# The opening transfers of a two-block transformer kernel, issued in another order and from other queues

## The chip, the cores and the metric

One core of one Trainium2 chip runs the whole program in one launch. The metric is the device time in microseconds (us); lower is better. The engines are TensorE (PE; its weight loads are listed as PEld), VectorE (DVE), ScalarE (ACT), GpSimd (POOL) and SyncE (SP). SP, ACT and POOL can issue DMA transfers; in the profile queue 1 is SP's, queue 10 is ACT's, queue 0 is POOL's.

## The reference

The input x is 256 rows of 1024 float32. Two blocks are applied to it: one with an attention layer beside a state-space mixer ("even"), a stick-breaking attention layer and two feed-forward layers, and one with a feed-forward layer, a gated and dilated mixing layer, cross attention to a memory and a last feed-forward layer. Only the first steps matter here:

```python
hn = rmsnorm(x, even_norm[i])
proj = hn @ even_w_in[i]                       # [256, 1024] @ [1024, 1280]
q, k, v, u = split(proj, ...)                  # u: the state-space mixer's input, 512 wide
# state-space mixer, G = 32 groups, N = 64 states, P = 16 channels
dt  = exp(log_dt)[:, None]
mag = exp(a_re * dt)
lam_re, lam_im = mag * cos(a_im * dt), mag * sin(a_im * dt)
bb_re, bb_im = (complex weight from lam and a) * (b_re, b_im)
h = associative_scan(lam, einsum(u, bb))       # over the 256 positions
y = einsum(h_re, c_re) - einsum(h_im, c_im)
```

## The kernel before, in words

Every engine has an instruction stream of its own, written out by hand, and they meet at semaphores. Matrices come from HBM in 1 MB "units" (128 partitions x 2048 float32) into `raw`, which has three buffers; `load` (L558 to L566) issues unit u on SP once buffer u mod 3 is free. The units of `even_w_in` are u0 to u0+4: columns 3 and 4 (the mixer's u), then 0, 1 and 2 (q, k, v).

SP (L552 on) issues x in one transfer (L554, semaphore `x_loaded`), the early constants with the identity (L555, 157.5 KB), the norm's gain (L556), units 0 to 2 (L622 to L623 through L566), 20 small loads (L625, `small_in`) and then units 3 and 4, which have to wait until TensorE is through with units 0 and 1. ACT (L1781 on) begins with seven transfers: `ssm_loads` (a_re, a_im and log_dt, which is broadcast to 128 partitions, 16 KB), `b_loads` (two matrices of 256 KB with what is broadcast, to partitions 0 to 63 of `bc_nat`) and `c_loads` (two of 128 KB, to partitions 64 to 127).

The opening computation: VectorE sums the squares of row half 0 of x (t = 0, L2221), ScalarE those of row half 1 (L1673), GpSimd makes the reciprocal roots (L1565, L1567), one row half after the other, once its memsets (L1542, L1544) are done. VectorE scales row half 0 (L2232) and half of row half 1 (L2234), ScalarE the other half (L1693). Ahead of that last scaling ScalarE waits for `ssm_in` and takes exp(log_dt) (L1792), from which VectorE makes the mixer's tables (L2439 on).

TensorE (L958 on) works in this order: it waits for the constants and for all three of `ssm_in`, flips a_re and a_im (L806), flips the scaled rows (`norm(0)`, 16 flips at L806), from which ScalarE makes `h_whole` (L1701); waits for `b_in` and flips B (32 flips at L806); multiplies unit 0 (`whole_t`, L713); waits for `c_in` and flips C (L982); multiplies unit 1 (L713); then flips and groups u, multiplies units 2 to 4 (L725) between the mixer's steps, and so on:

```python
norm(0)
pe.wait_ge(b_in, 16 * 2)
...
whole_t(u0, OUT["even_u0"], fresh=chunks(0))
pe.wait_ge(c_in, 16 * 2)
...
whole_t(u0 + 1, OUT["even_u1"])
```

VectorE copies the flipped B (L2451), and then works without long waits on the mixer's V and W products (L2481 to L2509); TensorE needs the last of them for the K product (L1061). GpSimd adds the skip term to it (L1590) and then SP, ACT and POOL move it in small transfers inside SBUF (L517) ahead of the convolution (L1098, L1101).

## Time and profile before

| | |
|---|---|
| median of three runs | 1208.72 us |
| lowest, highest | 1207.64, 1209.81 us |
| profiled execution: span from first to last instruction | 1208.6 us |
| busy: PE, DVE, ACT, POOL | 98%, 65%, 49%, 6% |
| unit 0: issued, landed | 2.27, 16.67 us |
| TensorE's first matmul on unit 0 | 16.71 us |

The profile is of one execution, whose whole time is given by its span alone. Times in its rows count from the first instruction. A busy TensorE isn't TensorE at its peak, since matmuls are pipelined; what a change is worth is read from the waits and from the chain of work that ended last. In a row of the timeline or of the groups, "out<-in" are the tiles written and read, xN is the number of instructions, and the bracket at the end is the idle time before them with what ended it.

### The profile page before, as it was taken

To read this page: it belongs to the slowest core of one execution; us is meant where nothing else is said; L and a number is where in the kernel's file an instruction comes from. 1 tells how busy PE (TensorE), PEld (TensorE's weight loads), DVE (VectorE), ACT (ScalarE), POOL (GpSimd) and SP (SyncE) were. 2 spreads that over 40 slices of the span, in tenths; PEclk is the share of its full clock that TensorE was granted. 3 is DMA by queue.
4 is the path that set the end of the run, shared out by engine and by line. 5 is a ranking of instruction groups with operands and counts; after the bars stand their busy time and mean duration, and the time that the engine had idled before them with its cause. 6 is when DMAs were issued, how large, how long until landed. Compare 5 with 4: busy or idle time off the path is not lost.

```text
span 1208.6 us, 17835 instructions
## 1 busy us (share of the span) xinstructions
PE 1185.3 (98%) x7139; PEld 1026.1 (85%) x7139; DVE 783.1 (65%) x848; ACT 588.8 (49%) x730; POOL 67.1 (6%) x87
## 2 busy tenths in 40 slices
PE   6999999999999999999999999999999999999997
PEld 5876888888999988888888888888889988888886
DVE  6956676666755557666667666667594646766665
ACT  4547643434566645434345444445574545443443
POOL 2120000000002110000000000000011000000000
PEclk9999999999999999999999999999999999999999
DMA  7254565656544355656555556565543534656561
GB/s 196 92 145 141 162 207 177 200 179 202 180 140 168 113 168 181 207 177 196 185 191 168 199 178 205 177 204 175 175 133 116 183 127 134 197 185 197 179 202 70
DMA packets 156104, 205.81 MB, mean 170 GB/s; under 512 B 7752, under 2 KB 129168, under 8 KB 156048
## 3 DMA queue, kind: packets, MB, share of 16 engines
q1 hardware_dynamic: 154944, 203.30, 52.2%
q10 hardware_dynamic: 944, 1.52, 0.6%
q8 instruction: 40, 0.66, 0.2%
q0 software_dynamic: 160, 0.20, 0.1%
q14 instruction: 16, 0.13, 0.0%
HBM read 202.77 MB, written 1.05 MB: 169 GB/s over the span
## 4 chain that ended last, share of the span: by engine, by line
PE 92%; DVE 3%; ACT 2%; DMA 1%; SPq 1%; issue 0%; POOL 0%; POOLq 0%; ACTq 0%
PE outp L754 26%; PE outp L695 20%; PE acc L695 20%; PE outp L758 14%; PE acc L806 3%; PE outp L713 1%; DMA raw<-in_even_w_in_dram 1%; PE outp L1193 1%; DVE w_lo L2198 1%; PE outp L725 1%; DVE h_pair L2243 1%; PE outp L860 1%; SPq L517 1%; PE acc L1173 1%; ACT w_hi L1650 0%; ACT h_pair L1711 0%
## 5 line engine op out<-in xcount | busy, mean ns | idle before, releaser
L1650 ACT ACTIVATE w_hi<-raw 128x2048 fp32r<-128x2048 f32 x177 | 339.4, 1918 | 413.0 <-PE outp L758 283.2
L2198 DVE TENSOR_TENSOR w_lo<-raw,w_hi 128x2048 fp32r<-128x2048 f32 x177 | 405.3, 2290 | 177.0 <-ACT w_hi L1650 176.9
L754 PE MATMUL outp<-h_pair,w_hi 128*128 128x512 f32 x1056 | 253.9, 391 | 0.3
L754 PEld LDWEIGHTS outp<-h_pair,w_hi 128*128 128x128 f32 x1056 | 195.0, 188 | 42.7 <-DVE h_pair L2243 4.2
L758 PEld LDWEIGHTS outp<-h_pair,w_lo 128*128 128x128 f32 x1056 | 135.4, 191 | 5.2
L695 PE MATMUL acc<-w_hi,f_lo 128*128 128x512 f32 x352 | 137.4, 390 | 0.0
L695 PE MATMUL acc<-w_hi,f_hi 128*128 128x512 f32 x352 | 137.4, 390 | 0.0
L695 PE MATMUL acc<-w_lo,f_hi 128*128 128x512 f32 x352 | 137.1, 389 | 0.0
L758 PE MATMUL outp<-h_pair,w_lo 128*128 128x256 f32 x1056 | 137.0, 283 | 0.0
L695 PE MATMUL outp<-w_hi,h_pair 128*128 128x512 f32 (+1 forms) x416 | 113.9, 361 | 0.3 <-DVE w_lo L2198 0.3
L2297 DVE TENSOR_REDUCE arena<-outp 128x256 f32<-128x512 f32 x88 | 56.7, 686 | 58.4 <-PE outp L758 56.2
L2310 DVE TENSOR_REDUCE arena<-outp 128x256 f32<-128x512 f32 x88 | 56.7, 686 | 56.4 <-PE outp L758 56.1
L695 PEld LDWEIGHTS outp<-w_hi,h_pair 128*128 128x128 f32 x416 | 73.1, 189 | 13.4 <-DVE w_lo L2198 1.4
L695 PEld LDWEIGHTS acc<-w_lo,f_hi 128*128 128x128 f32 x352 | 66.1, 188 | 14.0
L695 PEld LDWEIGHTS acc<-w_hi,f_hi 128*128 128x128 f32 x352 | 66.2, 188 | 12.7
L754 PE MATMUL outp<-m_pair,w_hi 128*128 128x512 f32 x320 | 76.7, 392 | 0.0
L695 PEld LDWEIGHTS acc<-w_hi,f_lo 128*128 128x128 f32 x352 | 66.2, 188 | 12.4
L695 PE MATMUL outp<-w_lo,h_pair 128*128 128x512 f32 (+1 forms) x208 | 74.2, 357 | 0.0
L695 PE MATMUL outp<-h_pair,w_hi 128*128 128x256 f32 x384 | 70.8, 286 | 0.0
L754 PEld LDWEIGHTS outp<-m_pair,w_hi 128*128 128x128 f32 x320 | 59.3, 188 | 12.5 <-issue 0.2
L695 PEld LDWEIGHTS outp<-h_pair,w_hi 128*128 128x128 f32 x384 | 59.8, 191 | 0.9 <-issue 0.5
L1565 POOL TENSOR_SCALAR arena<-arena 128x1 f32<-128x1 f32 x20 | 9.6, 481 | 907.3 <-ACT xn L1673 884.8
(340 smaller groups left out, 1438.7 us busy)
## 6 DMA issues: line engine op xcount, KB each, us to landing
raw<-in_ffn_w_gate_dram SPq DMA_DIRECT2D x44, 1024.0 KB, 5.6
raw<-in_ffn_w_up_dram SPq DMA_DIRECT2D x44, 1024.0 KB, 5.6
raw<-in_ffn_w_down_dram SPq DMA_DIRECT2D x44, 1024.0 KB, 4.9
raw<-in_odd_w_in_dram SPq DMA_DIRECT2D x12, 1024.0 KB, 5.2
raw<-in_w_in_dram SPq DMA_DIRECT2D x10, 1024.0 KB, 5.2
raw<-in_even_w_in_dram SPq DMA_DIRECT2D x5, 1024.0 KB, 14.4
raw<-in_even_w_out_dram SPq DMA_DIRECT2D x4, 1024.0 KB, 6.8
raw<-in_cross_wk_dram SPq DMA_DIRECT2D x4, 1024.0 KB, 5.7
```

The source lines that it names most:

```text
L517: eng.dma_start(m_in[PC * j:PC * j + PC, cc, S - 1 - j:, :, :], lags[32 * cc:32 * cc + PC, 0:j + 1, :, :]).then_inc(landed, 16)
L695: ins = nc.tensor.matmul(dst, lhs, rhs, start=start and n == 0, stop=stop_ and n == 2, skip_group_check=skip)
L713: ins = nc.tensor.matmul(outp[:, k % NB, m * L:(m + 1) * L], w[:, c, m * P:(m + 1) * P], h_f32[:, c, :], start=c == 0, stop=c == C - 1)
L725: ins = nc.tensor.matmul(outp[:, k % NB, t * UW:(t + 1) * UW], h_f32[:, c, t * P:(t + 1) * P], w[:, c, :], start=c == 0, stop=c == C - 1)
L754: nc.tensor.matmul(bank, w[0][:, c, m * P:(m + 1) * P], x[:, :, c, :], start=c == 0, stop=c == C - 1, skip_group_check=True)
L758: ins = nc.tensor.matmul(outp[:, (k + m) % NB, 0:L], w[1][:, c, m * P:(m + 1) * P], x[:, 0, c, :], start=False, stop=c == C - 1, skip_grou ...
L806: return nc.tensor.transpose(dst, src, ident[base:base + rows, base:base + rows])
L860: nc.tensor.matmul(outp[:, (k + m) % NB, :].rearrange("p (a l) -> p a l", l=L)[:, :, rows], w[:, c, m * P:(m + 1) * P], m_pair[:, :, c, ro ...
L1650: A(w_hi[:, slot(u), :], raw[:, u % RAW, :], ACT.Copy).then_inc(w_hi_ready, 1)
L2198: tt(w_lo[:, slot(u), :], raw[:, u % RAW, :], w_hi[:, slot(u), :].bitcast(F32), ALU.subtract).then_inc(w_lo_ready, 1)
L2297: V.reduce_sum(silu[:, j % 2, m * L:(m + 1) * L], bank.rearrange("p (a l) -> p l a", l=L), AX).then_inc(out_free[(k + m) % NB], 1)
L2310: V.reduce_sum(b[:, m * L:(m + 1) * L], bank.rearrange("p (a l) -> p l a", l=L), AX).then_inc(out_free[(k + m) % NB], 1)
```

## The change

x comes in two transfers, one for each row half, with a semaphore each; VectorE waits for the first, ScalarE for the second. The B transfers go from ACT's queue to SP's, between units 0 and 1, and the C transfers between units 1 and 2. log_dt gets its own semaphore and is issued by GpSimd ahead of its memsets; TensorE's first wait is then for a_re and a_im only, and ScalarE's wait ahead of the exponential is for log_dt alone. ACT keeps the two issues of a_re and a_im. The computation is the same.

```diff
@@ -355,11 +355,12 @@
         acc_ready = sem("acc_ready")
         acc_free = [sem(f"acc_free{i}") for i in range(NB)]
         out_free = [sem(f"out_free{i}") for i in range(NB)]
-        x_loaded, consts_in, late_in, late2_in, mem_in, fin_in = (sem("x_loaded"), sem("consts_in"), sem("late_in"),
+        x_loaded = [sem(f"x_loaded{t}") for t in range(T)]
+        consts_in, late_in, late2_in, mem_in, fin_in = (sem("consts_in"), sem("late_in"),
                                                                   sem("late2_in"), sem("mem_in"), sem("fin_in"))
         ssm_in, b_in, c_in, small_in, gain0_in = (sem("ssm_in"), sem("b_in"), sem("c_in"), sem("small_in"),
                                                   sem("gain0_in"))
-        bc_flipped = sem("bc_flipped")
+        bc_flipped, dt_in = sem("bc_flipped"), sem("dt_in")
         sum_ready, result_ready = sem("sum_ready"), sem("result_ready")
         act_step, dve_step, pool_step = sem("act_step"), sem("dve_step"), sem("pool_step")
         half_ready = sem("half_ready")
@@ -502,13 +503,13 @@
             return v.rearrange("(a n) -> a n", a=1)
         ssm_loads = [(a_raw[:, j, :, :], a[n][0].unsqueeze(1).to_broadcast([G, 2, N]))
                      for j, n in enumerate(["ssm_a_re", "ssm_a_im"])]
-        ssm_loads += [(log_dt, row(a["ssm_log_dt"][0]).to_broadcast([P, G]))]
         b_loads = [(bc_nat[G * j:G * j + G, :].rearrange("g (h m) -> g h m", h=2),
                      a[n][0].rearrange("g n p -> g (n p)").unsqueeze(1).to_broadcast([G, 2, 1024]))
                     for j, n in enumerate(["ssm_b_re", "ssm_b_im"])]
         c_loads = [(bc_nat[G * j + 64:G * j + 64 + G, 0:N * PC], a[n][0].rearrange("g p n -> g (p n)"))
                    for j, n in enumerate(["ssm_c_re", "ssm_c_im"])]
         SSM = len(ssm_loads)
+        dt_load = (log_dt, row(a["ssm_log_dt"][0]).to_broadcast([P, G]))
         m_moves = [(j, cc) for j in range(S) for cc in range(4)]
         M_SP, M_POOL, M_ACT = m_moves[:15], m_moves[15:20], m_moves[20:]
 
@@ -551,7 +552,8 @@
 
         @block.sync
         def _(sp):
-            sp.dma_start(x_sb[:, :, :], a["x"][0].rearrange("(t p) f -> p t f", p=P)).then_inc(x_loaded, 16)
+            for t in range(T):
+                sp.dma_start(x_sb[:, t, :], a["x"][0, t * P:(t + 1) * P, :]).then_inc(x_loaded[t], 16)
             sp.dma_start(early, a["consts"][:, 0:EARLY_W]).then_inc(consts_in, 16)
             sp.dma_start(gains[:, 0, :], a["even_norm"][0].rearrange("(p c) -> p c", c=C)).then_inc(gain0_in, 16)
 
@@ -619,8 +621,13 @@
             if "even" in running:
                 u0 = UNITS["even"]
                 w = by_p(a["even_w_in"][0])
-                for j, n in enumerate([3, 4, 0]):
-                    load(u0 + j, cols(w, n))
+                load(u0, cols(w, 3))
+                for dst, src in b_loads:
+                    sp.dma_start(dst, src).then_inc(b_in, 16)
+                load(u0 + 1, cols(w, 4))
+                for dst, src in c_loads:
+                    sp.dma_start(dst, src).then_inc(c_in, 16)
+                load(u0 + 2, cols(w, 0))
                 for dst, src in small_loads:
                     sp.dma_start(dst, src).then_inc(small_in, 16)
                 for j, n in enumerate([1, 2]):
@@ -1539,6 +1546,8 @@
         def _(pool):
             own = Own(pool, pool_step)
             gp = nc.gpsimd
+            if "even" in running:
+                gp.dma_start(*dt_load).then_inc(dt_in, 16)
             gp.memset(half, -0.5).then_inc(half_ready, 1)
             if "even" in running:
                 gp.memset(m_in.rearrange("p a b c d -> p (a b c d)"), 0.0).then_inc(kz_ready, 1)
@@ -1782,13 +1791,9 @@
                 u0, k0 = UNITS["even"], OUT["even"] - 2
                 for dst, src in ssm_loads:
                     nc.scalar.dma_start(dst, src).then_inc(ssm_in, 16)
-                for dst, src in b_loads:
-                    nc.scalar.dma_start(dst, src).then_inc(b_in, 16)
-                for dst, src in c_loads:
-                    nc.scalar.dma_start(dst, src).then_inc(c_in, 16)
-                act.wait_ge(x_loaded, 16)
+                act.wait_ge(x_loaded[1], 16)
                 squares(0, x_sb)
-                act.wait_ge(ssm_in, 16 * SSM)
+                act.wait_ge(dt_in, 16)
                 A(small[:, 0, :], log_dt, ACT.Exp).then_inc(dt_ready, 1)
                 norm_rows(0, x_sb)
                 act.wait_ge(lam_mag, 1)
@@ -2423,7 +2428,7 @@
 
             def even():
                 u0, k0 = UNITS["even"], OUT["even"] - 2
-                dve.wait_ge(x_loaded, 16)
+                dve.wait_ge(x_loaded[0], 16)
                 norm_front(0, x_sb)
 
                 k = ACC["prep_a"]
```

## Rows read from the trace of the kernel before

**Rows 1.** The page, part 4: shares of the chain that ended last, by engine.
```profile
PE 92%; DVE 3%; ACT 2%; DMA 1%; SPq 1%; issue 0%; POOL 0%; POOLq 0%; ACTq 0%
```

**Rows 2.** The chain in order of time, 0 to 60 us: start, duration, what.
```profile
2.27 14.40 DMA raw<-in_even_w_in_dram
...
16.71 10.14 PE outp L713 x32
26.85 2.00 PE outp L982 x128
...
57.91 2.14 PE outp L725 x9
```

**Rows 3.** Waits, 0 to 20 us: us in total, times, longest.
```profile
PE acc L806 <- DMA arena<-in_ssm_log_dt_dram: 9.7, 1, 9.7
...
PE outp L713 <- DMA raw<-in_even_w_in_dram: 1.1, 1, 1.1
```

**Rows 4.** Timeline of the opening: start, us, engine, line, operation, count, idle before.
```profile
0.86 3.51 POOL L1544 MEMSET arena_end<- 128x4096 f32 x1
...
2.27 9.22 SPq L566 DMA_DIRECT2D raw<-in_even_w_in_dram  x3
...
3.13 0.57 ACTq L1786 DMA_DIRECT2D arena<-in_ssm_b_im_dram  x1
...
5.99 0.69 DVE L2221 CUSTOM_DVE_ANT_0 xn<-x_sb 128x512 f32<-128x512 f32 x1 [5.99 <-DMA x_sb<-in_x_dram]
...
8.55 0.86 POOL L1565 TENSOR_SCALAR arena<-arena 128x1 f32<-128x1 f32 x1
...
10.04 3.68 PE L806 MATMUL acc<-arena,xn 128*128 128x128 f32 x16
...
12.54 3.03 ACT L1701 ACTIVATE h_whole<-acc,arena 128x256 f32<-128x256 f32 x8 [0.50 <-PE acc L806]
...
13.65 1.97 PE L806 MATMUL outp<-arena 32*128 32x32 f32 x32
...
26.95 0.58 SPq L566 DMA_DIRECT2D raw<-in_even_w_in_dram  x1
```

**Rows 5.** DMA issues of 0 to 5 us: KB each, us from issue to landing.
```profile
DMA packets 300, 0.92 MB, mean 184 GB/s; under 512 B 80, under 2 KB 80, under 8 KB 300
...
arena<-in_ssm_b_im_dram ACTq DMA_DIRECT2D x1, 256.0 KB, 10.5
...
arena<-in_ssm_log_dt_dram ACTq DMA_DIRECT2D x1, 16.0 KB, 7.8
```

**Rows 6.** DMA by stretch (last columns: share, GB/s), and queue 10 of 8 to 12 us.
```profile
3.00:6.00 3.00, 0.00 (x0) 0.00 (x0) 0.01 (x1) 1.09 (x1) 1.37 (x1) 1.00 1.01 373
6.00:8.00 2.00, 0.00 (x0) 0.00 (x0) 1.30 (x4) 1.53 (x5) 0.41 (x2) 1.00 0.61 127
...
q10 hardware_dynamic: 234, 0.67, 69.3%
...
14.00:20.00 6.00, 4.90 (x38) 4.14 (x37) 4.88 (x9) 5.58 (x13) 0.00 (x0) 1.00 1.10 343
```

**Rows 7.** Matmuls of L713 by stretch (count in brackets).
```profile
16.70:20.10 3.40, 3.38 (x8) 2.76 (x9) 1.00 1.10 348
...
28.85:35.90 7.05, 7.05 (x32) 5.92 (x32) 1.00 0.44 144
```

**Rows 8.** All engines by stretch around 50 us (PEclk is the granted clock).
```profile
50.80:54.20 3.40, 3.40 (x21) 3.40 (x20) 3.33 (x3) 2.38 (x6) 0.00 (x0) 0.61 0.00 0
```

**Rows 9.** Timeline, 58 to 71 us.
```profile
58.64 2.47 DVE L2509 TENSOR_TENSOR arena<-arena,xn 128x1536 f32<-128x1536 f32 x1
...
64.27 2.04 PE L1061 MATMUL acc<-arena 128*16 128x128 f32 x64
...
68.18 2.71 POOL L517 DMA_DIRECT2D arena_end<-arena  x5 [0.31 <-POOL arena L1590]
```

**Rows 10.** DMA issues of 67.9 to 80 us: GpSimd's transfers, us to landing.
```profile
arena_end<-arena POOLq DMA_DIRECT2D x4, 40.0 KB, 2.6
```

## The prediction

> **What bounds the kernel now.** The page's chain that ended last comes first: 92% of it is TensorE [rows 1], so a change at the opening can give back only what TensorE waits there, and what it gains has to survive every later hand-over. Next comes the chain in order of time [rows 2]: a DMA piece of the first weight unit, 2.27 to 16.67 us, and from 16.71 on TensorE without a gap: unit 0 (10.14 us), C matrices (2.00), then unit 1, 7.1 [rows 7]. The waits [rows 3] give its idle time before that: 9.7 us until log_dt is in, since L806 asks for all three small SSM loads, and 1.1 us for unit 0. The timeline [rows 4] fills in the rest. The norm's 16 flips end at 13.72, the 32 flips of the B matrices run 13.65 to 15.62 (their input lands at 3.13 + 10.5 = 13.6 [rows 4, 5]), ScalarE has h ready at 15.57, then comes the gap to 16.71. TensorE's order is fixed: norm, B flips, unit 0, C flips, unit 1. So the start of unit 0 is the later of two things, its own landing and the B landing plus about 2.07 us (1.97 of flips and two hand-overs). Before, the first decides by 1.1 us.
>
> **Part by part.**
> x in two halves. The 1 MB lands at 5.99 [rows 4] and moves at 373 GB/s [rows 6], so its second half takes 0.52 MB / 373 GB/s = 1.4 us and the first is in near 4.6. VectorE's sum for row half 0 and the first scale move by up to 1.4 us. Row half 1 doesn't land earlier; its GpSimd pair, L1565 at 8.55, waits for ScalarE's squares and the first pair, and I put it 1.0 us earlier. The price is one more issue on SP, about 0.5 us like the issue of b_im in [rows 4], ahead of unit 0, whose packets wait for x's anyway: nothing.
>
> log_dt by GpSimd. ScalarE loses one issue and, with B and C gone, four more, of about 0.5 us each, all ahead of its squares; those still wait for row half 1 near 6.0, so this is worth 0.2 us at most. TensorE's first flips no longer need log_dt. On GpSimd an issue costs 2.71 / 5 = 0.54 us [rows 9] and lands 2.6 us later [rows 10]; with 128 rows say 1 us and 3 to 8 us (the old way took 7.8 [rows 5]). Behind it stands the 3.51 us memset, which then ends near 5.0 to 5.4, before the first sum is ready at 6.0: nothing. ScalarE waits for it at L1792, ahead of half of row half 1's scaling, at about 8.9: hidden if it lands by then.
>
> So the norm's flips end 1.7 to 2.2 us sooner, near 11.5 to 12.0, and ScalarE's 3.03 us of h [rows 4] end near 14.3, following the flips. None of this sets the end alone, since B comes between.
>
> Unit 0 and B. Before, B and C (0.79 MB) were on ScalarE's queue, and while they ran (8 to 12 us) that queue held 69.3% of the DMA time for 0.67 MB [rows 6]; unit 0 crawled. Now unit 0 has the engines to itself. By 5.0 us 0.92 MB had moved [rows 5], by 8.0 another 0.37 + 0.25 [rows 6], 1.54 together; less x, constants, gain (1.21) and some 0.1 of queue 10, 0.2 MB of unit 0 was in. The slow stretch of 6 to 8 us (127 GB/s [rows 6]) I keep, as x, constants and gain still stand ahead of it. The other 0.85 MB at the 343 GB/s of plain weight traffic [rows 6] take 2.5 us: last byte at 10.5. B is 0.52 MB behind it. Its rate alone on the engines no row shows. The near bound is queue 10's 0.67 MB in 0.693 x 4 us = 242 GB/s, that is 2.2 us; the good bound is x's 373 GB/s, with rows of the same 4 KB, 1.4 us; the bad one is 3.1 us, the 0.67 MB in 4 us that queue 10 made beside unit 0. I take 2.2, for it is the same transfer to the same 64 partitions. From last byte to landing I allow 0.4 us: x's bytes were through near 5.4 (0.92 MB at 5.0, 373 GB/s), and it landed at 5.99. So B is in at 13.1. B now decides, not unit 0: flips 13.15 to 15.1, unit 0's matmuls from 15.15 in place of 16.71. **Gain 1.6 us.** With the good bound, and the slow stretch 1 us shorter, B would be in at 11.3, the norm's flips (12.0) and ScalarE's h decide, and the gain is 2.7; with the bad bound (0.9 us more) and 0.7 us more in front it is 0.
>
> The Trainium skill, "SBUF — State Buffer" (the DMA port swizzle), says that partitions 0 to 63 reach only 8 of the 16 ports, so that such a transfer gets half the bandwidth, by its figure 218 GB/s. That speaks against the change, for B alone leaves half the ports idle where before unit 0 ran beside it. An estimate by that page is 2.4 us in place of 2.2, a gain of 1.4. The row's 242 agrees with it more than x's 373 does.
>
> Unit 1 and C. Unit 1 lands 3.1 us (1.05 MB / 343) after B, near 16, and C by 17.5; both are wanted at 25.2 or later. Cover is 7 us, so nothing. Small loads, unit 3 and what follows on SP: the issue of unit 3 stood at 26.95, right behind the last small load [rows 4]. If SP gets through its list no sooner, unit 3 is still issued 29 us before its first matmul near 56 (57.9 before [rows 2]). Nothing.
>
> **Whether the 1.6 us reach the end.** VectorE starts its long run behind the B flips, which end only 0.6 us sooner. Its last W product ended at 61.11 and TensorE wanted it at 64.27 [rows 9], so 3.2 us of cover lose 1.0 and 2.1 remain. From K on, GpSimd, SP's moves and the convolution follow TensorE. I find no wait that eats the gain.
>
> **The clock.** The granted clock reads 1.00 at 16.7 us, but the pace doesn't: 8 matmuls of L713 in 3.4 us against 32 in 7.05 later [rows 7], 0.42 against 0.22 us, so unit 0 begins at the lower level (1.2 GHz) and costs 10.14 - 7.1 = 3.0 us more than warm. If the rise keeps its distance to TensorE's start, nothing changes. If it keeps its instant, the 1.6 us won hold 3.9 slow matmuls that are worth 0.85 us. If it comes earlier, as TensorE now runs from flips into unit 0 without the 1.1 us gap, up to 3.0 more are to be had. A second dip lies at 50.8 to 54.2 (0.61 [rows 8]), worth at most 0.39 x 3.4 = 1.3 us, and may move or vanish. I take the first case and keep 1 us either way.
>
> The sum against the profiled execution: 1208.6 - 1.6 = 1207.0; its span stands 0.1 us below the median 1208.72 of the runs. Against the median the forecast is 1207.1.
>
> **Rivals.**
> A, the forecast: B's landing is the new gate, gain 0.8 to 2.4. For it: bytes and rates above. Chance 0.55, 1207.1.
> B, more than the landing: the slow stretch shrinks, or the clock rises before half of unit 0 is through. 1.6 + 1.2 = 2.8 us off, 1205.9. For it: fewer small transfers from a second queue in 6 to 8 us, TensorE busy earlier without a gap. Against it: x, constants and gain still stand first. Chance 0.22.
> C, exchange of one wait for another: bytes ahead of the B flips are nearly all the old ones, so B lands at 13.6 to 14.6 (13.6 before) and the 1.1 us gap only turns into a wait ahead of the flips; or the clock's instant stays. Gain 0 to 0.8, 1208.4. The Trainium skill, "DMA: Bandwidth & Descriptors" (issuing engines are not separate DMA queues), says that moving transfers between queues saves issue time alone; by it this case gains weight. Against it: C's bytes and unit 1's no longer run ahead of B. Chance 0.17.
> D, slower: log_dt. If GpSimd's 128 rows of 128 bytes are served behind unit 0 and B, they land after 13. ScalarE then stands at L1792 with norm_rows, the second half of the norm and h behind it: Exp 0.2, scaling 0.7, flips 1.9, B flips 2.0 and hand-overs, 5.0 us from log_dt to unit 0. It decides from a landing at 11.7; at 13.5 the time is 1.8 us over the old one, 1210.5, more at a later landing. Against it: 2.6 us from issue to landing [rows 10]. Chance 0.06.
> That the queue change does nothing is contained in C.
>
> **How the numbers follow.** About 0.2% (2.4 us) is what a measurement of this kernel can tell from no change. A lies inside, B mostly beyond, C inside, D partly beyond. Faster 0.22, same 0.73, slower 0.05. The likeliest case gives 1207.1. The range 1205.4 to 1209.0 holds A, C and the near part of B, and leaves out B's far end (0.1) and D with a noisy C (0.1).
>
> **What would show it.** Right: VectorE's first sum near 4.6 to 5.0; TensorE's first flips before 8; the norm flips over by 12; a wait of about 1 us of the B flips on in_ssm_b_im and none of L713 on even_w_in; L713 from 15.1; then the same pieces 1.6 us earlier up to 100 us. Wrong: L713 before 14.5 (the slow stretch was the other queue's doing), or L713 at 16 or later, B's rate being lower; ScalarE waiting on log_dt past 9.5; unit 0's 32 matmuls taking another length than 10.1 us, which would be the clock; or TensorE waiting for VectorE near 62.

## The result, and the profile after

| | kernel before | changed kernel |
|---|---|---|
| median of 15 runs each | 1208.98 us (1207.48 to 1211.24) | 1211.54 us (1210.56 to 1212.77) |
| ratio | | 1.0021, 95% interval 1.0014 to 1.0028 |
| profiled execution, span | 1208.6 us | 1209.8 us |

The change makes the kernel 2.5 us slower (0.0021 x 1209); the forecast was 1207.1, with 1209.0 as the upper end of the range. The profiled execution of the changed kernel took 1211.54 us with a span of 1209.8; in all the runs that follow, too, 1.7 to 1.9 us lie outside the span. A "flip" is a transpose on TensorE; unit 0 is the first 1 MB of weights.

The chain in order of time, changed kernel, 0 to 62 us (start, duration, what), the answer to [rows 2]:

```profile
4.06 11.39 DMA arena<-in_ssm_b_im_dram
15.49 1.98 PE outp L813 x28
17.47 9.02 PE outp L720 x32
26.49 2.00 PE outp L989 x128
28.49 7.11 PE outp L720 x32
...
57.04 1.95 PE acc L1039 x64
```

The chain now begins with a B matrix, not with the first weight unit. B is in at 4.06 + 11.39 = 15.45 us, 1.85 later than before (13.6 [rows 4, 5]) and 2.35 later than forecast. The waits of TensorE, 0 to 30 us, beside [rows 3]:

```profile
PE acc L813 <- DMA arena<-in_consts_dram: 8.2, 1, 8.2
PE outp L813 <- DMA arena<-in_ssm_b_im_dram: 3.2, 1, 3.2
```

The 9.7 us for log_dt and the 1.1 for unit 0 are gone. In their place stand 8.2 us for the constants and 3.2 for B. The timeline of the opening, beside [rows 4]:

```profile
1.32 0.80 POOL L1550 DMA_DIRECT2D arena<-in_ssm_log_dt_dram  x1 [0.82 <-POOLq L2852]
...
4.57 0.69 DVE L2226 CUSTOM_DVE_ANT_0 xn<-x_sb 128x512 f32<-128x512 f32 x1 [4.57 <-DMA x_sb<-in_x_dram]
...
7.72 0.23 ACT L1797 ACTIVATE arena<-arena 128x32 f32<-128x32 f32 x1 [0.42 <-DMA arena<-in_ssm_log_dt_dram]
...
8.58 3.68 PE L813 MATMUL acc<-arena,xn 128*128 128x128 f32 x16
...
11.08 3.03 ACT L1710 ACTIVATE h_whole<-acc,arena 128x256 f32<-128x256 f32 x8 [0.45 <-PE acc L813]
...
15.49 1.98 PE L813 MATMUL outp<-arena 32*128 32x32 f32 x32 [3.23 <-DMA arena<-in_ssm_b_im_dram]
```

Everything ahead of B is as early as planned: the first half of x is in at 4.57, the norm's flips are over at 12.26, ScalarE has h at 14.11. Then TensorE stands until 15.49. DMA by stretch (last columns: share of the engines' time, GB/s), beside [rows 6]:

```profile
6.00:8.00 2.00, 0.00 (x0) 0.00 (x0) 0.75 (x1) 1.53 (x5) 1.40 (x3) 1.00 0.70 205
8.00:10.00 2.00, 1.77 (x9) 1.71 (x10) 1.24 (x5) 0.72 (x1) 0.57 (x2) 1.00 1.13 383
10.00:12.00 2.00, 2.00 (x11) 1.86 (x9) 1.73 (x9) 1.49 (x5) 0.00 (x0) 1.00 1.07 194
12.00:15.00 3.00, 0.26 (x2) 0.00 (x0) 1.24 (x5) 2.98 (x8) 0.00 (x0) 1.00 1.08 158
```

Unit 0 alone streams at 383 GB/s (8 to 10 us). From 10 to 15 us, with B, the rate falls to 194 and 158 GB/s at a share of 1.07, so the engines are not idle but slow. The packet records of the same trace, counted in the half microsecond in which a packet ended (number of packets, mean ns of one; some of the half microseconds):

```
until us   rows of 1 KB (units 0, 1)   rows of 4 KB (B)    GB/s
  9.0          190   46                   -                 389
 10.0          121   51                  11  183            338
 11.0           33  106                  12  371            166
 12.0            9   88                  21  344            191
 13.0           35  109                  12  340            170
 14.0           41  138                   8  452            150
 15.0           85  109                   1  427            182
 15.5          157   58                   -                 322
```

x, with rows of the same 4 KB into all 128 partitions, took 198 ns for one packet; a packet of B takes 341 ns in the mean, up to 514. B's first packet starts at 9.43 us, while unit 0 is still running: of its 1024 rows at most 930 were through by 10.0, the last not before 11.5, and it landed at 12.4. B's last packet ends at 14.61, and B lands 0.84 us behind it. So its 128 packets spread over 5.2 us, although 16 engines with 8 each at 341 ns would be done in 2.7 (an estimate). When the last of them ended, 226 rows of unit 1 were through as well. The records don't name the engine; I read the counts so: engines that are through with their share go on to unit 1's rows (over 100 ns each behind 12.5 us), while the last engines still carry B. Why some are so far behind the others, no run tells. The Trainium skill, "DMA: Bandwidth & Descriptors" (two DMAs through the same engine are not ordered), says that nothing orders DMAs across the 16 engines; the counts agree, B and both its neighbours in the line run side by side.

The last part is the clock. Unit 0's matmuls took 9.02 us in place of 10.14 [rows 2], as the granted clock rose at 21.3 us, 3.8 behind their start, and in the profile of before at 22.75, 6.0 behind it. In this profile the low stretch near 50 us was twice as long as in [rows 8] (all engines by stretch; last columns PEclk, DMA share, GB/s):

```profile
48.70:52.10 3.40, 3.40 (x21) 3.33 (x21) 3.33 (x3) 1.95 (x4) 0.00 (x0) 0.50 0.11 38
52.10:55.50 3.40, 3.40 (x18) 3.40 (x17) 3.33 (x3) 2.37 (x5) 0.00 (x0) 0.51 0.00 0
```

So the gap between the two profiles runs 0.8 us at unit 0's start (17.47 against 16.71), -0.4 at its end, 1.1 at the state product (57.04 against 55.96) and 1.2 at the end. The rest of the 2.5 us is in the profile of before itself, below.

### The profile page after: what moved, and what is told of

It is laid out like the page before. It is cut to its first block, busy times and chain, and to the rows that moved or that the text cites. A ratio compares the mean times of both kernels' runs of the same rounds, so it can differ in the third digit from the quotient of the medians.

```text
span 1209.8 us, 17836 instructions
## 1 busy us (share of the span) xinstructions
PE 1185.7 (98%) x7139; PEld 1026.9 (85%) x7139; DVE 783.2 (65%) x848; ACT 589.0 (49%) x730; POOL 66.7 (6%) x88
## 4 chain that ended last, share of the span: by engine, by line
PE 92%; DVE 3%; ACT 2%; DMA 1%; SPq 1%; issue 0%; POOL 0%; POOLq 0%; ACTq 0%
PE outp L761 26%; PE outp L702 20%; PE acc L702 20%; PE outp L765 13%; PE acc L813 3%; PE outp L720 1%; PE outp L1200 1%; DMA arena<-in_ssm_b_im_dram 1%; DVE w_lo L2203 1%; PE outp L732 1%; DVE h_pair L2248 1%; PE outp L867 1%; SPq L518 1%; PE acc L1180 1%; ACT w_hi L1659 0%; ACT h_pair L1720 0%
## 5 line engine op out<-in xcount | busy, mean ns | idle before, releaser
L702 PEld LDWEIGHTS acc<-w_hi,f_lo 128*128 128x128 f32 x352 | 66.2, 188 | 12.3
L761 PEld LDWEIGHTS outp<-m_pair,w_hi 128*128 128x128 f32 x320 | 59.3, 188 | 12.5 <-issue 0.2
```

The source lines that it names most:

```text
L702: ins = nc.tensor.matmul(dst, lhs, rhs, start=start and n == 0, stop=stop_ and n == 2, skip_group_check=skip)
L761: nc.tensor.matmul(bank, w[0][:, c, m * P:(m + 1) * P], x[:, :, c, :], start=c == 0, stop=c == C - 1, skip_group_check=True)
```

## The experiments

One table for all, from the profiles (us) and the timed runs. "Released by" names what TensorE waited for right before, with the wait; "flips" means that it came from the work ahead of it without a wait. The runs of the kernel before on the same chips had medians of 1208.98 to 1209.52.

| kernel | B flips from, released by | unit 0 from, released by | K product | median (runs) | ratio, 95% |
|---|---|---|---|---|---|
| before | 13.65, flips | 16.71, weights 1.1 | 64.27 | 1208.98 (15) | |
| before, again | 13.01, flips | 15.21, weights 0.3 | 61.48 | 1207.3 (1) | |
| changed | 15.49, B 3.2 | 17.40, flips | 65.35 | 1211.54 (15) | 1.0021 [1.0014, 1.0028] |
| changed, again | 15.70, B 3.4 | 17.61, flips | 64.99 | 1212.0 (1) | |
| B and C moved alone | 18.28, B 5.1 | 20.18, flips | 66.96 | 1212.39 (9) | 1.0025 [1.0015, 1.0035] |
| x halves alone | 12.11, flips | 15.20, weights 1.1 | 62.88 | 1209.37 (11) | 0.9997 [0.9988, 1.0006] |
| log_dt alone | 13.16, flips | 15.67, weights 0.5 | 63.24 | 1209.21 (11) | 0.9995 [0.9986, 1.0004] |
| B and C back | 15.04, flips | 16.94, flips | 62.56 | 1210.6 (11) | 1.0009 [1.0000, 1.0018] |
| B over both partition halves | 14.27, B 2.0 | 16.15, flips | 63.87 | 1210.29 (11) | 1.0006 [0.9997, 1.0015] |
| log_dt by ScalarE | 15.55, B 3.7 | 17.46, flips | 64.24 | 1211.78 (11) | 1.0017 [1.0008, 1.0026] |
| B once | 13.31, B 1.2 | 17.11, flips | 64.58 | 1211.37 (11) | 1.0019 [1.0010, 1.0028] |
| B ahead of unit 0 | 12.46, flips | 14.37, flips | 62.20 | 1207.95 (11) | 0.9992 [0.9983, 1.0001] |
| B ahead, log_dt by ScalarE | 11.69, flips | 13.60, flips | 61.18 | 1207.11 (11) | 0.9983 [0.9974, 0.9992] |
| the same, constants between x's halves | 13.97, flips | 15.88, flips | 63.34 | 1209.24 (11) | 1.0001 [0.9992, 1.0010] |
| x halves, log_dt and B by ScalarE, spread | 11.70, flips | 14.88, weights 1.2 | 62.14 | 1208.85 (11) | 0.9993 [0.9984, 1.0002] |
| x halves, B once by ScalarE | 11.48, flips | 15.40, flips and weights at once | 62.95 | 1208.88 (11) | 0.9997 [0.9988, 1.0006] |
| before with idle matmuls | 14.62, flips | 16.50, flips | 62.55 | 1209.19 (11) | 0.9999 [0.9990, 1.0008] |

The starts come from one profile each, by its timeline (in the chain the changed kernel's unit 0 starts at 17.47), the medians from all the timed runs. In the 17 profiles the time of the profiled execution is the start of the K product plus 1145.8 to 1147.2 us (for the first profile of before, the span plus 1.7 is taken as its time). So what the opening wins or loses by then is carried to the end, and the K product is the place to read it.

### Which part costs: one alone, or one undone

**B and C moved alone.** The kernel before with the B and C lines of the diff and nothing else.

> The kernel before with one part of the change alone: B and C go to SP's queue between the units; x in one transfer and log_dt on ScalarE's queue as before. Theory 1 (B in line): B lands near 15 to 15.5 us, because it is slow behind unit 0, TensorE waits ahead of the B flips for over 1 us, and the whole is 1 to 2.5 us slower than the kernel before. Theory 2 (log_dt through GpSimd): the slow packets of log_dt are what delays everything; without them B lands by 13.5 and the time is that of before or up to 1.5 us less. Theory 3 (clock): the opening is neutral and the loss is made near 50 us; then this kernel has the second clock dip 6.8 us long and loses 1 to 1.5 us there.

1212.39 us, 1.0025. The cost is all there without the other two parts. The chain of this kernel:

```profile
3.73 14.51 DMA arena<-in_ssm_b_im_dram
18.28 1.98 PE outp L811 x28
20.25 9.31 PE outp L718 x32
```

B needs 14.51 us from issue to landing. It is in at 18.2, 2.8 us later than in the changed kernel and well behind the 15 to 15.5 expected; unit 0 landed later too, at 14.9 against 12.4. This profiled run was the slowest of its nine (1213.47), so the 18.28 is at the late end; what else delayed both is open.

**x halves alone**, the kernel before with the x_loaded lines.

> The kernel before with x in two halves alone. Additive theory: x and log_dt together cost 1.1 us in bc_back, where the constants landed at 11.0; if log_dt through GpSimd is the whole of it, x alone costs nothing: VectorE's first sum near 4.8, L713 from 16.5 to 16.9, time within 0.5 us of before. Rival: the halves themselves delay what stands behind them, then constants land past 8 here too and the time is over 0.7 us above before.

**log_dt alone**, the kernel before with dt_load on GpSimd.

> The kernel before with log_dt by GpSimd alone. If its long packets on all 16 engines hold up the constants (as in bc_back: 1.70 to 11.0 us), the constants land at 8 to 11 us, TensorE's first flips start then, L713 starts at 16.9 or later and the time is 0.5 to 1.5 us above before. Rival: it needs the halves of x as well; then constants by 6.7 and the time of before or 0.3 us less.

Both measure as no change (0.9997 and 0.9995). TensorE's flips are earlier, but the weights of unit 0 remain the gate (1.1 and 0.5 us), as in the kernel before. With log_dt alone the constants did land late, at 8.5, as expected, and yet neither the late unit 0 nor the loss of 0.5 to 1.5 us came: TensorE waited until 8.9 for a_im, another of the small loads.

**B and C back**: the changed kernel with B and C on ScalarE's queue again.

```
-                for dst, src in b_loads:
-                    sp.dma_start(dst, src).then_inc(b_in, 16)
...
+                for dst, src in b_loads:
+                    nc.scalar.dma_start(dst, src).then_inc(b_in, 16)
```

> The changed kernel with B and C back on ScalarE's queue; x in halves and log_dt by GpSimd stay. Theory 1: unit 0 gates again as before (16.5 to 17), the norm's flips stay early (over by 12.3), the time is within 1 us of the kernel before. Theory 2: log_dt's slow packets still delay unit 0, L713 starts at 17.5 or later and the time is over 1 us above before. Theory 3: the time follows the length of the dip near 50 us, one window of 3.4 us as before or two, whatever the opening does.

1.0009, some 1.5 us less than the changed kernel, but not level with before. The first wait tells why; the last line is a new one, near 62 us:

```profile
PE acc L808 <- DMA arena<-in_consts_dram: 11.1, 1, 11.1
...
PE acc L1063 <- issue: 1.0, 1, 1.0
```

The constants landed only at 11.0 us, and the norm's flips were over at 15.1, not by 12.3. The trace has log_dt's 16 KB from GpSimd as 16 packets of 1 KB, 13 of which took 1.0 to 1.8 us each (a 1 KB row of a weight unit: 46 ns); up to 15 of them were under way at once, so they held nearly all of the 16 DMA engines, and the constants' rows ran among them. By ScalarE the same bytes go as 128 packets of 128 bytes at 12 ns. That is not the whole of it: log_dt's last packet ended at 7.4, the constants' last row at 9.5, with B on the other queue from 5.6 on, and with log_dt by GpSimd alone the constants landed at 8.5. What makes up the rest is open.

### What makes B late

**B over both partition halves**: b_im in partitions 64 to 95 and c_re in 32 to 63, so that the four matrices use both halves of the 128 partitions.

```
-        b_loads = [(bc_nat[G * j:G * j + G, :].rearrange("g (h m) -> g h m", h=2),
+        b_loads = [(bc_nat[64 * j:64 * j + G, :].rearrange("g (h m) -> g h m", h=2),
```

> The changed kernel with b_im in partitions 64 to 95 and c_re in 32 to 63 (before: b_im 32 to 63, c_re 64 to 95); same bytes, same order. Theory 1 with the ports of the Trainium skill (SBUF page) as its cause: B is written through both halves of the ports and lands 1.5 to 2.5 us earlier (13 to 14 against 15.45), unit 0 starts near 15.5, the time is 1 to 2 us under the changed kernel's. Rival: B is slow for its place in line or its few partitions per engine; then it lands at 15 to 15.5 as before and the time is the changed kernel's.

B lands at 14.22, 1.2 us sooner, a little less than expected; one packet of it takes 288 ns in place of 341. The Trainium skill, "SBUF — State Buffer" (the DMA port swizzle), says that partitions 0 to 63 reach only 8 of the 16 ports; the direction agrees, and the spread is worth 1.2 us of the 2.35 that B is over its forecast. It leaves B as the gate. On ScalarE's queue the same spread did little: B at 10.6 against 10.9 and unit 0 at 14.8 against 15.15 us (x halves, log_dt and B by ScalarE, spread, against x halves alone).

**log_dt by ScalarE** in the changed kernel, with a semaphore of its own.

```
-            if "even" in running:
-                gp.dma_start(*dt_load).then_inc(dt_in, 16)
...
+                nc.scalar.dma_start(*dt_load).then_inc(dt_in, 16)
```

> The changed kernel with log_dt issued on ScalarE's queue behind a_re and a_im, semaphores as in the change. Theory 2: the 16 packets of 1.1 to 1.6 us vanish, the constants land by 6.7 (8.2 in the changed kernel), unit 0 and B land 1 us or more earlier, the time is over 1 us under the changed kernel's. Theory 1: the packets cost the constants only; B lands within 0.5 us of 15.45 and the time is within 0.7 us of the changed kernel's.

The constants land 1.5 us sooner (6.7 against 8.2), B not at all (15.51). As long as B gates, constants that land sooner are worth nothing.

**B once**: each B matrix loaded once, 0.26 MB in place of 0.52. The flips read the one copy twice.

```
-                        ins = flip(outp[:, (OUT["even_b"] + j) % NB, p * G:(p + 1) * G],
-                                   bc_nat[G * j:G * j + G, p::PC], G, G * j)
+                        rows = slice(G * j, G * j + G)
+                        for h in range(2):
+                            ins = nc.tensor.matmul(outp[N * h:N * h + N, (OUT["even_b"] + j) % NB, p * G:(p + 1) * G],
+                                                   bc_nat[rows, p:1024:PC], ident[rows, rows],
+                                                   start=True, stop=True)
```

> The changed kernel with each B matrix loaded once in place of twice (0.26 MB in place of 0.52); the flips read the one copy twice, as 64 small matmuls in the form of the C flips. Theory (B moves at 158 to 194 GB/s behind unit 0, and its bytes are what it costs): B lands 1.3 to 1.7 us sooner, near 14.0, TensorE waits 1.7 us in place of 3.2, unit 0 starts near 16.0 and the time is about 1210.1. Rival (B is late because of the 1 KB packets and the rows of unit 0 ahead of it, not by its own bytes): B lands at 15 or later, and the time stays at 1211 to 1212.

Half the bytes bring B in 2.2 us sooner (4.10 + 9.16 = 13.26), more than expected, so its own bytes are a large part of what delays it. The time shows nothing of it, as twice the number of flips took 3.88 us in place of 1.98:

```profile
4.10 9.16 DMA arena<-in_ssm_b_im_dram
13.31 3.88 PE outp L979 x111
17.18 8.54 PE outp L719 x32
```

I had read the C flips (2.07 us for 128 records) as the price; with a source that steps over 16 elements the same count costs 3.88. The step is not shown as the cause: the granted clock rose at 20.06 us in this trace, behind these flips and ahead of the C flips. Against the clock speaks only that the 32 flips of B in the old form, with the same step, took 1.95 us behind an early rise (the kernel with idle matmuls) and 1.97 ahead of it. The time alone would have spoken for the rival; the landing speaks against it.

**B ahead of unit 0**: the decisive one. The order within the one queue is all that differs from the changed kernel.

```
-                load(u0, cols(w, 3))
                 for dst, src in b_loads:
                     sp.dma_start(dst, src).then_inc(b_in, 16)
+                load(u0, cols(w, 3))
```

> The changed kernel with the two B transfers ahead of the first weight unit on SyncE's queue, everything else as changed. Theory (the place in the line is what costs, since B's bytes stand behind 1.05 MB): B lands at 9 to 11 us and never gates, TensorE goes from the norm's flips (over near 12.3) into the B flips, and unit 0, now behind B, lands at 13.5 to 14.5; its matmuls start at 14.5 to 15, 2.5 us before the changed kernel's 17.47, and the time is about 1209, no slower than before. Rival (the sum of bytes in one line at the slow rate is what costs, and their order doesn't matter): unit 0 lands where B landed, at 15.5 or later, its matmuls start at 15.5 to 17, behind a wait of L720 for the weights of 1.5 us or more, and the time is 1210 to 1211.

1207.95 us, 0.9992: the loss is gone, and the interval just reaches 1.0001, so that it is not shown to be faster than the kernel before. The only wait of TensorE in the first 30 us is that for the constants, 8.5 us. The timeline:

```profile
12.46 1.97 PE L813 MATMUL outp<-arena 32*128 32x32 f32 x32
14.37 8.98 PE L720 MATMUL outp<-h_whole,raw 128*128 128x256 f32 x32
```

DMA by stretch:

```profile
8.00:10.00 2.00, 1.50 (x8) 1.44 (x9) 1.13 (x4) 0.72 (x1) 0.69 (x2) 1.00 1.02 186
10.00:12.00 2.00, 2.00 (x11) 2.00 (x10) 1.76 (x9) 1.21 (x4) 0.00 (x0) 1.00 1.08 252
12.00:15.00 3.00, 3.00 (x37) 2.52 (x36) 1.77 (x7) 2.98 (x9) 0.00 (x0) 1.00 1.10 349
```

B is as slow here (186 GB/s), but it runs mostly from 7 to 10.5 us and lands at 11.3, beside TensorE's wait for the constants and the norm's flips. Unit 0 behind it lands at 14.2, 0.2 us before TensorE asks for it. The rival, that only the sum of bytes counts, wanted it at 15.5 or later and is out.

### The two kernels once more

**The kernel before, one more profile.**

> The kernel before itself, one more profile, to see how much of the clock's places is a matter of the run. Theory: the first rise of the granted clock and the low stretch near 50 us move by a microsecond or more, or the low stretch doubles or vanishes, with unit 0's start at 16.3 to 16.8 and no other change; then differences of 1 to 1.3 us between two profiles that come from those stretches say nothing of the kernels. Rival: all stretches stand within 0.3 us of the first profile's (rise 22.7, low 50.05 to 53.46), and they belong to the kernel.

```profile
PE acc L806 <- DMA arena<-in_ssm_log_dt_dram: 8.7, 1, 8.7
PE outp L713 <- DMA raw<-in_even_w_in_dram: 0.3, 1, 0.3
```

This run took 1207.3 us and had unit 0 start at 15.21, 1.5 us before that of [rows 2], with log_dt in 1.0 us sooner than in [rows 3]. Its clock was low from 16.2 to 19.7 and from 46.96 to 50.37. The state product came 2.8 us sooner than in the first profile and the end 3.0, with no edit between them. The part of the theory on the clock holds; that unit 0 would start at 16.3 to 16.8 does not. Not only the clock, the landings of the opening are a matter of the run too.

**The changed kernel, one more profile.**

> The changed kernel itself, one more profile, to set beside the second profile of the kernel before, in which unit 0 began 1.5 us sooner than in the first. Theory (the cost belongs to B's place in the line): B lands at 15 to 15.6 us again, TensorE waits 3 us or more for it, and unit 0 starts at 17.1 to 17.6. Rival (the landing of B is a matter of the run as the landing of unit 0 is in the kernel before): B lands 1 us or more away from 15.45.

B in right before 15.70, a wait of 3.4 us, unit 0 at 17.61. B's late landing came again.

### What can be gained at the opening

**B ahead, log_dt by ScalarE**: the two findings together.

> The changed kernel with B ahead of the first weight unit, and log_dt issued by ScalarE (with its own semaphore) instead of GpSimd. Theory (GpSimd's 16 slow packets hold the constants, which in the kernel with B first alone landed at 8.5 us and set the start of TensorE's flips): the constants land near 6.7, as in the other kernel with log_dt on ScalarE, the norm's flips are over by 11.5 in place of 12.5, B's by 13.5, and unit 0 starts at 13.5 to 14.4, whichever of flips and weights is later; the time is 0.4 to 1 us under that of B first alone, about 1207.5. Rival (log_dt's queue is worth nothing once B is in front): the constants at 8 us or later, unit 0 at 14.3 or later, the time within 0.3 us of B first alone.

1207.11 us, 0.9983 [0.9974, 0.9992]: faster than the kernel before by 2.1 us and, by the two ratios, than the changed one by 4.6 (0.0038 x 1209). Timeline of TensorE:

```profile
7.74 0.42 PE L813 MATMUL acc<-arena 32*128 32x32 f32 x2 [7.74 <-DMA arena<-in_consts_dram]
8.08 3.68 PE L813 MATMUL acc<-arena,xn 128*128 128x128 f32 x16
11.69 1.97 PE L813 MATMUL outp<-arena 32*128 32x32 f32 x32
13.60 8.73 PE L720 MATMUL outp<-h_whole,raw 128*128 128x256 f32 x32
```

The constants still come later than I expected (7.7, not 6.7), 0.8 us sooner than with log_dt on GpSimd, and unit 0 starts 0.77 us sooner. Against B ahead alone the two ratios differ by 1.1 us, but their intervals overlap, so that this last step is not clear of noise.

**The same, constants between x's halves**, and B and C spread.

```
+            sp.dma_start(x_sb[:, 0, :], a["x"][0, 0:P, :]).then_inc(x_loaded[0], 16)
             sp.dma_start(early, a["consts"][:, 0:EARLY_W]).then_inc(consts_in, 16)
+            sp.dma_start(x_sb[:, 1, :], a["x"][0, P:2 * P, :]).then_inc(x_loaded[1], 16)
```

> As the kernel with B first and log_dt by ScalarE, and besides the constants between the two halves of x, and B and C spread over both halves of the partitions. Theory (what sets unit 0's start is now its own 1.05 MB behind x, constants and 0.52 MB of B): constants at 5 to 6, half 1 of x some 0.5 us later than before (6.5), unit 0 lands at 13 to 13.5 and its matmuls start right then, 1 us before B first alone; if the granted clock and VectorE's W products allow, the time is 1207; where VectorE's W products decide (the K product waits at about 62), no better than B first alone. Rival (spread partitions and the constants' place do nothing): unit 0 at 14.3 or later.

A miss. The constants are in at 5.4, but the second half of x only at 8.5, against 6.0 in the changed kernel; I had put 6.5:

```profile
8.48 0.63 ACT L1680 ACTIVATE xn<-x_sb 128x512 f32<-128x512 f32 x1 [4.99 <-DMA x_sb<-in_x_dram]
...
11.65 1.12 PE L813 MATMUL acc<-arena,xn 128*128 128x128 f32 x4 [2.14 <-DVE arena L2435]
```

The second half of the norm hangs on it, and TensorE stands twice for 2.1 us. The 2.5 us are much more than 157 KB of constants; its last packet ended at 7.1, so 1.4 of them lie behind the bytes. Why, no run here tells, and as B and C were spread in the same run, the constants' place is not shown as the cause.

**x halves, log_dt and B by ScalarE, spread**: B and C on ScalarE's queue as before, over both partition halves, x in halves, log_dt with a semaphore of its own.

> x in halves, log_dt on ScalarE's queue with a semaphore of its own, B and C on ScalarE's queue as before, but b_im in partitions 64 to 95 and c_re in 32 to 63. Port theory: B lands by 12.8 and unit 0 by 15.5 (16.67 before), L713 starts near 15 to 15.5 and the time is 0.7 to 1.7 us under before. Rival (bytes and line alone count): B and unit 0 land as before, 13.6 and 16.7, and the time is that of before within 0.5 us.

**x halves, B once by ScalarE.**

> The kernel before with x in halves, log_dt on ScalarE's queue with a semaphore of its own, B and C on ScalarE's queue as before, and each B matrix loaded once (0.26 MB less in all). Theory (bytes ahead of the later of unit 0 and B set the start): B lands near 9 to 10, unit 0 at 13.9 to 14.5 (it was 0.26 MB later in the earlier kernel with x halves, 15.2), and unit 0's matmuls start at 14.2 to 14.6, gated by the norm's and B's flips or by a short wait for the weights. Of the 2.3 us against before the VectorE's W products leave about 2, the time is 1207.5 to 1208.5. Rival (the clock and the VectorE floor eat every gain at the opening): unit 0 starts as early, but the time is 1209 to 1209.5.

0.9993 and 0.9997, neither of them told from no change. In the first, unit 0's weights gate again (1.2 us). The second is a miss: 0.26 MB less were to bring unit 0 in at 13.9 to 14.5, and it landed at 15.36, just as the doubled flips ended (15.35). With x halves alone, and all the bytes, it was in at 15.15, so fewer bytes of B brought unit 0 in no sooner on this queue.

**Before with idle matmuls**: 13 matmuls of 128x128 by 128x256 on zeros ahead of the first flips, to have the clock up when unit 0 starts.

```
+                pe.wait_ge(kz_ready, 1)
+                idle_w = m_in.rearrange("p a b c d -> p (a b c d)")
+                for _ in range(13):
+                    nc.tensor.matmul(outp[:, 3, 0:256], idle_w[:, 0:P], idle_w[:, 0:256], start=True, stop=True)
                 pe.wait_ge(consts_in, 16)
```

> The kernel before with 13 extra matmuls of 128x256 on zeros (a memset tile, into a PSUM bank that nothing uses yet) while TensorE waits for its first data, 4.4 to 9.7 us; nothing reads their result. Clock theory: the granted clock has risen before unit 0, whose 32 matmuls take 7.2 us in place of 10.14, and the norm's flips under 3.7; the time is 1.5 to 3 us under before. Rival: the clock falls back in the waits ahead of B and unit 0, unit 0 takes over 9 us and the time is within 0.7 us of before. The dip near 50 us should stay in both.

```profile
4.42 8.07 PE L963 MATMUL outp<-arena_end 128*128 128x256 f32 x26 [4.42 <-POOL arena_end L1548]
12.42 0.31 PE L806 MATMUL acc<-arena 32*128 32x32 f32 x2
...
16.50 7.17 PE L713 MATMUL outp<-h_whole,raw 128*128 128x256 f32 x32
23.61 2.07 PE L986 MATMUL outp<-arena 32*64 32x32 f32 x128
```

Unit 0 takes 7.17 us in place of 10.14, as the higher level (2.4 GHz) would have it [rows 7], and the C flips come 3.2 us sooner than in the first profile of before, 0.4 sooner than in the second. The 1.5 to 3 us that were expected do not come: 0.9999. The wait ahead of the K product and VectorE's last W product say where it went:

```profile
PE acc L1065 <- issue: 1.3, 1, 1.3
...
60.69 1.76 DVE L2513 TENSOR_TENSOR arena<-arena,xn 128x1536 f32<-128x1536 f32 x1
```

VectorE ends its W products at 62.45, and K starts at 62.55. In 16 of the 17 profiles that end lies 45.45 to 45.60 us behind the end of the B flips: 61.11 - 15.62 before, 62.93 - 17.47 in the changed kernel, 59.12 - 13.66 with B ahead and log_dt by ScalarE, 62.46 - 17.01 with B and C back (45.9 with the idle matmuls). TensorE's way from the start of unit 0 to K is 45.6 to 47.9 us, by what the clock does; the two shortest, 45.6 and 46.05, have the waits of 1.0 and 1.3 us in them. So where unit 0 follows the B flips without a gap, a faster clock gains at most some 2 us (47.9 - 45.6, an estimate) before VectorE decides, and only earlier B flips move both.

## Why the prediction was wrong

**The failed step: the price of B behind unit 0.** The text put the last byte of unit 0 at 10.5 and B's 0.52 MB behind it at 242 GB/s, 2.2 us, landing at 13.1, with 168 GB/s (3.1 us) as the bad bound. The packets give each term. B started sooner than forecast, at 9.4 in place of 10.5, beside the tail of unit 0, whose own last row came no sooner than 11.5 (forecast 10.5). But it took 5.2 us from first to last packet (101 GB/s) in place of 2.2, and landed 0.84 us behind its last packet in place of 0.4: -1.1 + 3.0 + 0.4 = 2.3 us late, 15.45 against 13.1. The 242 GB/s were the rate of a whole queue beside another one; by the counts above, what B gets as one piece in a line is set by the last of 16 engines, while the others are on unit 1 already. Both bounds were averages over engines. Unit 0's matmuls so began at 17.47 and not at 15.15: 2.3 us of the miss, and the text's own sign of being wrong, "L713 at 16 or later, B's rate being lower". Moving the same two transfers ahead of unit 0, in the same queue, takes the loss back, with C left in its place; so it is B's place in the line and not the queue. Half the bytes (2.2 us) and partitions in both halves (1.2 us) bring B in sooner too, but leave it as the gate. The kernel with B and C moved alone shows that the loss needs neither of the other parts.

**The base.** The sum stood against the span of 1208.6 and called it 0.1 us below the median. But 1.7 us lie outside the span, so that the profiled execution took some 1210.3 us, 1.6 above the median of 1208.72. The second profile shows what was special: unit 0 at 15.21, a wait of 0.3. The 1.6 us that were to be gained were thus, as far as two profiles can tell, largely a late opening of one run. Over the table, medians follow unit 0's start (13.6 us and 1207.1, 14.4 and 1207.95, 16.15 and 1210.3, 17.4 and 1211.5), and the level of the kernel before, 1209.0 to 1209.5, belongs to starts of 14.9 to 15.9. Off that line lie the idle matmuls (16.5 and 1209.2), whose clock is faster, B and C back (16.9 and 1210.6) and B and C moved alone (20.2 and 1212.4). The forecast's own start of 15.15 would have been little or no gain. With 2.3 us for B and 1.6 for the base, 1207.1 becomes 1211.0; the last 0.5 us is of the size of the clock's moves, and no run assigns it. In the text's sum for the clock, 1.6 us hold 3.8 slow matmuls worth 0.77 us, not 3.9 worth 0.85; the forecast does not rest on it.

**Right.** x in halves (4.6 forecast, 4.57), log_dt in time (3 to 8, it was 7.7), the norm's flips over at 12.26 where 11.5 to 12.0 was forecast, ScalarE's h at 14.1 (14.3), no wait for unit 1 or C, VectorE's cover kept. That these parts are worth nothing while something behind them gates is shown by the two runs of a part alone. **Half right:** "TensorE's first flips no longer need log_dt" holds, but the constants took its place at 8.2, where the text wanted the first flips before 8; log_dt's own packets are the likely cause, as with x in halves and log_dt by GpSimd they landed at 8.0 to 8.5 us in five profiles of four kernels (11.0 with B and C back), and with log_dt by ScalarE at 6.7 to 7.7 in five; the text had costed the GpSimd issue on its queue and in its landing, and nothing on the DMA engines that it shares. With B ahead of unit 0 that moved unit 0's start by 0.8 us.

**The two cited rules.** The Trainium skill, "SBUF — State Buffer", would have had B 0.2 us slower than the row, by the prediction's estimate; the trace went the same way, by far more. The rule of the Trainium skill, "DMA: Bandwidth & Descriptors" (issuing engines are not separate DMA queues), that another queue saves issue time alone was counted for rival C. It doesn't hold for this kernel in the sense that matters: the queue and the place in it decide what a transfer stands behind, and B and C alone, moved to the other queue, cost 3.0 us (0.0025 x 1209).

**The rivals.** The result came by none of them. C named the right exchange (a wait ahead of the B flips in place of one for the weights), but let B land no later than 14.6. D had the right sign by the wrong transfer: log_dt landed at 7.7, long before the 11.7 at which it would decide.

**The clock.** The text let the rise keep its distance to TensorE's start, and kept 1 us either way. That was the right size: unit 0 took from 8.5 to 10.2 us over the kernels without idle matmuls, and the profiles show none, one or two low stretches of 3.4 us at about 0.5 near 50 us.

## What to carry to other kernels

As this kernel shows it, a transfer that gates belongs ahead of the large ones in its line, above all a slow one to a part of the partitions, and its price is the time from its first packet to its last on the slowest engine, with what follows it mixed in; an average rate of a stretch is no bound for it. Before a gain of a microsecond is forecast from one profile, ask how that profile's own time, span and what lies around it together, stands to the median, and whether the wait to be removed is there in another run. Two kernels that differ at the opening are best told apart by the start of the first piece that nothing hides, here unit 0, and then by the first piece that needs another engine's long run, here the K product, whose start the times of all the profiles follow within 1.4 us.

## What the runs showed that I had not expected

- A broadcast load of 16 KB issued by GpSimd moved as 16 packets of 1 KB, most of them at 1.0 to 1.8 us each and up to 15 at once; by ScalarE as 128 packets of 128 bytes at 12 ns. With it the constants were later by 0.8 us (7.7 against 8.5, B ahead) to 1.5 us (6.7 against 8.2).
- With 157 KB of constants between the halves of x, and B and C spread, the second half came 2.5 us later (8.5 against 6.0). Open.
- The same kernel, profiled twice, had unit 0's start at 16.71 and 15.21 us.
- 128 records of a flip whose source steps over 16 elements took 3.88 us, the C flips, with a contiguous source but at the higher clock, 2.07. Step and clock are not told apart.
- VectorE's last W product ended 45.45 to 45.60 us behind the end of the B flips in 16 of 17 profiles, whatever the opening and the clock did.
- 26 records of the idle matmuls at the start took 8.07 us, 0.31 each; unit 0's later 32 of the same size 0.22 each.
